# Holding back the second half of a head pair until the token transposes of the next pair's preparation

## What is computed

```python
A = eye(G_CHUNK) + einsum('nbhid,nbhjd->nbhij', kb, kc) * dec_strict
sol = triangular_solve(A, rhs, left_side=True, lower=True, unit_diagonal=True)
def step(S, inp):
    u_b, w_s, qk_n, q_n, k_n, dec_n = inp
    u = u_b - w_s @ S
    o = q_n @ S + qk_n @ u
    return dec_n * S + k_n.T @ u, o
S, o = lax.scan(step, S0, ...)
o = o * rsqrt(mean(o * o) + G_NORM_EPS) * norm_g * silu(z)
```

## Time and profile before

| | us |
|---|---|
| three runs, median (lowest to highest) | 2825.7 (2819.3 to 2831.36) |
| the profiled execution, its own time | 2820.61 |
| its span | 2818.5 |
| PE busy | 2602.7 (92%) |
| DVE busy | 1666.7 (59%) |
| ACT busy | 932.5 (33%) |

### The profile page before, as it was taken

The page is one execution under the profiler, slowest core; times in us unless marked ns, Lnnn a source line. Parts: engine busy times, 40 slices in busy tenths (PEclk is TensorE's granted clock), DMA queues, the critical chain, the costliest instruction groups (busy, mean ns, idle before and its releaser), DMA issues.

```text
span 2818.5 us, 59235 instructions
## 1 busy us (share of the span) xinstructions
PE 2602.7 (92%) x23238; PEld 2450.9 (87%) x23238; DVE 1666.7 (59%) x2503; ACT 932.5 (33%) x1683; POOL 161.2 (6%) x168
## 2 busy tenths in 40 slices
PE   8999999978877999999899999999787789999997
PEld 7999999866665899999899999988566668999996
DVE  5666437665667466663366663476657665666534
ACT  4333224342222243332233332334322223333323
POOL 1030110000000010001100001100000001000011
PEclk9999999987888999999999999999877889999997
DMA  4853324310000323233223223341000022232231
GB/s 111 100 96 87 90 82 125 94 33 5 10 10 23 98 75 89 82 87 90 76 85 88 83 88 87 104 135 46 29 2 9 10 74 70 82 89 83 86 90 58
DMA packets 380501, 201.67 MB, mean 72 GB/s; under 512 B 41461, under 2 KB 376821, under 8 KB 379528
## 3 DMA queue, kind: packets, MB, share of 16 engines
q1 hardware_dynamic: 377928, 197.46, 24.4%
q0 software_dynamic: 2400, 1.82, 2.0%
HBM read 188.07 MB, written 13.34 MB: 71 GB/s over the span
## 4 chain that ended last, share of the span: by engine, by line
PE 76%; DVE 11%; issue 5%; ACT 5%; DMA 1%; SPq 1%; DVEq 0%; ACTq 0%; POOLq 0%; POOL 0%
PE ps L683 55%; PE ps L738 20%; DVE ar L1939 3%; ACT ar L1430 2%; DVE ar L1933 2%; DVE wl L1817 1%; ACT wh L1358 1%; SPq L530 1%; PE ps L1014 1%; DMA raws<-in_ffn_w_in 0%; DVE x L1933 0%; DVE ar L1969 0%; DVE xl L1924 0%; DMA raws<-in_w_in 0%; DVE ar L1936 0%
## 5 line engine op out<-in xcount | busy, mean ns | idle before, releaser
L1817 DVE TENSOR_TENSOR wl<-raws,wh 128x1024 fp32r<-128x1024 f32 x336 | 411.3, 1225 | 671.4 <-ACT wh L1358 667.1
L683 PE MATMUL ps<-xh,wh 128*128 128x272 f32 x2880 | 605.8, 292 | 17.6 <-DVE wl L1817 15.0
L683 PE MATMUL ps<-xh,wl 128*128 128x272 f32 x2880 | 599.9, 290 | 0.0
L683 PE MATMUL ps<-xl,wh 128*128 128x272 f32 x2880 | 598.7, 289 | 0.0
L738 PE MATMUL ps<-ar 64*64 64x64 f32 (+12 forms) x5408 | 415.4, 267 | 133.4 <-ACT ar L1430 37.3
L738 PEld LDWEIGHTS ps<-ar 64*64 64x64 f32 (+5 forms) x5408 | 310.9, 155 | 215.9 <-issue 58.2
L1358 ACT ACTIVATE wh<-raws 128x1024 fp32r<-128x1024 f32 x336 | 354.7, 1057 | 415.8 <-PE ps L683 377.6
L683 PEld LDWEIGHTS ps<-xh,wh 128*128 128x128 f32 x2880 | 458.2, 190 | 21.0 <-DVE wl L1817 17.1
L683 PEld LDWEIGHTS ps<-xl,wh 128*128 128x128 f32 x2880 | 458.3, 190 | 0.0
L683 PEld LDWEIGHTS ps<-xh,wl 128*128 128x128 f32 x2880 | 457.5, 190 | 0.0
L683 PE MATMUL ps<-hh,wh 128*128 128x272 f32 x1408 | 292.2, 289 | 0.0
(11 more groups left out here) (194 smaller groups left out, 2659.7 us busy)
## 6 DMA issues: line engine op xcount, KB each, us to landing
raws<-in_ffn_w_in SPq DMA_DIRECT2D x176, 512.0 KB, 3.7
raws<-in_ffn_w_out SPq DMA_DIRECT2D x64, 512.0 KB, 4.0
raws<-in_w_in SPq DMA_DIRECT2D x42, 512.0 KB, 3.7
raws<-in_ffn_w_out SPq DMA_DIRECT2D x32, 384.0 KB, 3.4
raws<-in_w_out SPq DMA_DIRECT2D x16, 448.0 KB, 4.1
x_kept<-x SPq DMA_DIRECT2D x2, 2176.0 KB, 10.1
x<-x_kept SPq DMA_DIRECT2D x2, 2176.0 KB, 8.0
ar<-in_consts SPq DMA_DIRECT2D x2, 1337.5 KB, 6.6
```

The lines of the kernel that those rows point to most:

```text
L683: ins = pe.matmul(ps[:, bank + h, 0:n1 - h * NH], w[u % 2][:, k, :], a[:, k0 + k, h * NH:n1], start=(first and k == 0 and n == 0), stop=(l ...
L1817: dve.tensor_tensor(wl[u % 2][:, :, :], raw[u % 2][:, :, :], wh[u % 2][:, :, :].bitcast(F32), ALU.subtract).then_inc(sem("wl_done"), 1)
```

## The change

In stages 1 to 3 the finish no longer takes its first turn after the preparation's first step. All its 22 steps are spread evenly over the part of the scale that begins with the preparation's token transposes. The preparation's own steps keep their order, and the two other stages are as they were.

```diff
+STEPS_BEFORE_TOKENS = (6, 6 + GATE_STEPS, 9, 9)
-def alternate(first, n_first, second, n_second, second_over=1):
+def alternate(first, n_first, second, n_second, second_over=1, second_from=0):
-    order = sorted([((k + 1) / n_first, 0) for k in range(n_first)] + [((k + 1) / n_second * second_over, 1) for k in range(n_second)])
+    order = sorted([((k + 1) / n_first, 0) for k in range(n_first)]
+                   + [(second_from + (k + 1) / n_second * (second_over - second_from), 1) for k in range(n_second)])
...
-        alternate(prepare(q + 1), PREPARE_STEPS[q + 1], finish(q), FINISH_STEPS)
+        alternate(prepare(q + 1), PREPARE_STEPS[q + 1], finish(q), FINISH_STEPS, second_from=STEPS_BEFORE_TOKENS[q + 1] / PREPARE_STEPS[q + 1])
```

## The result

The changed kernel takes 2882.36 us (median of 4 runs, 2878.44 to 2884.85); the kernel before, on the same chip, 2828.53 (4 runs). The ratio is 1.0189, with a 95% interval of 1.0151 to 1.0226: slower by 54 us, where 2848 was forecast, 20 to 25 us slower, and 2870 was the upper end. The direction was right, the size was more than double. The profiled execution took 2884.85 us (span 2882.8). PE is busy 2621.4 us (2602.7 before), DVE 1670.6 and ACT 930.8, both as before.

The account below looks back on a forecast made before the run. PE bounds the late halves, a DVE-ACT-PE chain the early ones, and stage ends are paid in full. 12.7 + 9.9 - 10.1 = 12.5 us a layer, +25 in two layers: 2848 us, range 2826 to 2870.

Parts of the forecast that it names:

- The early halves: Each stage up to its first token transpose: finish steps leaving it save 7.4, 1.9 and 0.8, together 10.1 us a layer.
- The end of a stage: Behind the last level: F21 queues after the corner's copies on ACT, Newton comes later, together 9.9 us a layer.
- The Trainium skill's larger number: Stage ends: a table-set switch takes up to 2.66 us with drain; tail some 1.4 us longer, 8 us in all.
- the weight blocks that ACT takes behind stage 3: Loads issued behind F18 in stage 3: costed at nothing; without cover up to 3 us a layer.
- The late halves: Tokens, grams and inverse: moved finish steps add 4.8, 4.8 and 3.1, together 12.7 us a layer; bounds 8.4 and 21.7.
- Slower still: Rival: late half's clock rises later; each 5 us more at 1.2 GHz costs 15 in all, 2863 us; chance 0.15.
- The reason that I gave against it: Against "Slower still": with a clock of 0.58, the early half of stage 1 is near the lower level already.

Follow-up runs that it names:

- the first repair: Changed kernel with the finish's table load, Ln and Exp (F21) one step earlier on ScalarE, ahead of the corner's copies: 2865.3 us, ratio 1.0152.
- both repairs: Changed kernel with 33 extra unread products in the early halves of stages 2 and 3, and F21's rsqrt ahead of the corner's copies on ScalarE: 2846.87 us.

## Why the prediction was right and where it was wrong

**The early halves**: right. 10.1 us a layer was forecast and 11.2 measured, 8.0, 2.1 and 1.1 against 7.4, 1.9 and 0.8.

**The end of a stage**: right, 9.9 forecast, 10.6 measured, and the first repair gave 8.2 of it back. The Trainium skill's larger number ("ScalarE: Activation LUTs", What ACT_TABLE_LOAD costs) adds a drain of some 1.4 us to the load. Here the load of 1.28 us starts 0.02 us behind the corner's copies and Ln, at 856.30, 0.01 us behind its end, so that this case shows none. What the sum put at nothing, the weight blocks that ACT takes behind stage 3, cost nothing: ACT starts on them at 947.97, 0.6 us behind the start of xh, as before the change.

**The late halves**: the step that failed is the term "Added: 4.8, 4.8 and 3.1, together 12.7 us a layer". 27.9 were measured, beyond its own upper bound of 21.7. The step priced F2 to F7 by PE time at full clock, with the granted clock of the late half left where the earlier trace rows had it. By length times clock the work it spoke of is 13.0 us, near its value, though by stage it is 7.1, 4.6 and 1.3 against 4.8, 4.8 and 3.1, so that the match of the sums is partly luck. The other 14.9 are the clock. The prediction had this as the rival "Slower still", and two things were wrong with it. The price: it gave the clock 5 us more at 1.2 GHz in each stage, worth 15 us in all, where by the rows it is about 2, 12 and 16 us more in the three stages, worth 30 in all. And the place: it stood outside the sum, with a chance of 0.15, where the runs show it as a term of the sum. With its size by the rows 2848 + 30 is 2878.

**The reason that I gave against it** was the weak one. "The early half of stage 1 is near the lower level already" is true, and the clock does start the tokens low before too. What changed is when it rises. In stage 3 before, PE had the pieces of F3 and F6 among the preparation's products, 8.9 us of work in the last 16.8, and the clock rose about 4 us behind the first token transpose; after the change PE worked 5.7 us and it rose after 20, in both layers. It is a matter of chance as well: with 5.9 us it rose after 3.7 once, and in the order of before, with 8.8, after 16 once. I had counted the small products of the finish as work that waits for cheap time, and not as what may keep the clock near its rise.

**What is shown and what is not.** Shown by runs: that filling PE's idle time ahead of the tokens gives stage 3 its full clock and most of the lost time back (41.7 in place of 48.3 us, in both layers), that the tail is the order on ACT, that the two add to 35.5 us, and that clock alone moves one and the same half by 5.3 to 5.8 us. Not shown: that the idleness which the change makes there is enough for the 20 us at 1.2 GHz. Of four late halves of stage 3 that begin behind 5.6 to 6.0 us of work, three had it and one didn't. Only bookkeeping, and of one execution: the split 13.0 to 14.9; with the clock full in stage 3, 1.4 of the 7.9 us did not come back, so that a part of what I call clock is waiting that the slow clock had covered. Open: what makes the clock fall in the middle of a late half, as in stage 2 from 815 on. The changed kernel has new waits there (DVE makes two masks, 1.4 us together, ahead of the copy that F8's products need, and PE stands 1.96 us for it in stage 1), but a kernel that removes these waits alone wasn't tried. Open too is which part of the 21 us that remain with both repairs is moved work and which is these waits.

## What to carry to other kernels

In a phase of small matmuls with dependencies, interleaved work can also be what keeps TensorE's clock up: before moving it away to shorten a chain, look at the granted clock in short stretches around the place it leaves, and price the phase behind it at both levels, as a term of the sum and not as a rival. Multiply length by clock to see whether a stretch got more work or a slower clock; busy time doesn't tell. Look at the same piece in both layers and in several kernels before you trust a difference of some us in one trace. And a moved step takes its place in every engine's queue: read the new order on each engine near the end of a stage, where nothing hides a late table load.

## What the runs showed that I had not expected

One program can be granted different clocks at the same instructions: 0.50 or 1.00 in the same 8 us of stage 1, and run times from 2813.7 to 2842.3 us for one kernel, in step with the mean clock. The Trainium skill ("TensorE: Matmul & The Clock Gate", What's actually happening) says that what watches PE's activity runs freely and doesn't start with the kernel, so that the point of the rise varies from run to run; these runs fit that, and the spread is worth 1% here, with the rise moving in the middle of a kernel.

Pulling the finish ahead (2877.8 us) costs as much as holding it back (2882.4), both at a mean clock of 0.932 in the profiled execution against 0.942: of the orders tried, the even interleaving of before stands between two dearer ones.
